# Sparse attention of eight head pairs: the same instructions of three engines in another order

## The reference, cut to what matters

```python
sc = jnp.einsum('bqghd,bngd->bghqn', qg, k_cmp) * scale              # 31 compressed keys
p_cmp = softmax(where(valid_c, sc, NEG)) * any(valid_c)
o_cmp = jnp.einsum('bghqn,bngd->bqghd', p_cmp, v_cmp)
...
p_sel = softmax(where(valid_s, ss, NEG)); o_sel = p_sel @ v_sel      # causal, keys k_slc
p_w = softmax(where(valid_w, sw, NEG));   o_win = p_w @ v_win        # causal, keys k_win
...
out = jnp.einsum('bsch,bschd->bshd', gates, o).reshape(b, s, NSA_HEADS * DH)
return out @ w_o
```

## Time and profile before

| | |
|---|---|
| three runs | 2616.98, 2619.18, 2621.26 us |
| median | 2619.18 us |
| span of the profiled execution | 2617.9 us (its time is recorded as this span alone) |
| busy in the span | PE 2422.9 (93%), DVE 1367.0 (52%), ACT 988.3 (38%), POOL 1048.6 (40%) |
| the stage, from the first scores to the first product of the output projection | 853.53 to 1036.08 us, 182.6 us |

### The profile page before, as it was taken

One profiled execution on the slowest core, in us unless ns is written; L12 is line 12 of the kernel. 1 busy time (PEld: TensorE's weight loads), 2 busy tenths in 40 slices (PEclk: granted clock), 3 DMA queues, 4 the chain that ended last, 5 costly groups with the idle time before them and its releaser, 6 DMA issues.

```text
span 2617.9 us, 37191 instructions
## 1 busy us (share of the span) xinstructions
PE 2422.9 (93%) x13933; PEld 1920.0 (73%) x13933; DVE 1367.0 (52%) x2006; ACT 988.3 (38%) x1828; POOL 1048.6 (40%) x977
## 2 busy tenths in 40 slices
PE   6999899999999898999999799989999899899995
PEld 5777688888576555788888688869978797555553
DVE  3334254335364775344434656661167642588885
ACT  3344322222211665322223333341145401268784
POOL 7554444444006004544443645435741276401111
PEclk8999999999999999999999899999999899899998
DMA  4111233323233000333331211112210122399996
GB/s 132 57 49 57 84 100 95 98 89 104 65 102 92 1 1 9 104 98 96 96 97 41 77 41 44 47 49 73 81 33 27 31 89 76 130 308 362 366 369 234
DMA packets 267869, 268.51 MB, mean 103 GB/s; under 512 B 13339, under 2 KB 198518, under 8 KB 267750
## 3 DMA queue, kind: packets, MB, share of 16 engines
q1 hardware_dynamic: 262998, 253.91, 30.2%
q0 software_dynamic: 4752, 12.98, 1.9%
HBM read 256.10 MB, written 10.75 MB: 102 GB/s over the span
## 4 chain that ended last, share of the span: by engine, by line
PE 76%; DVE 9%; ACT 6%; DMA 5%; issue 3%; POOL 1%; SPq 0%; DVEq 0%; POOLq 0%; ACTq 0%
PE psum L2745 16%; PE psum L2749 16%; PE psum L2748 16%; DMA ex_tile<-in_w_down 4%; PE psum L1504 3%; PE psum L2388 2%; PE psum L844 2%; PE psum L2454 2%; PE psum L846 2%; PE psum L845 2%; PE psum L2260 1%; PE psum L2397 1%; ACT probs_a L1344 1%; ACT probs_b L1344 1%; PE psum L2265 1%
## 5 line engine op out<-in xcount | busy, mean ns | idle before, releaser
L2745 PE MATMUL psum<-x_hi,w_hi 128*128 128x264 f32 (+1 forms) x1536 | 525.5, 342 | 28.9 <-DVE x_lo L765 18.8
L2748 PE MATMUL psum<-x_lo,w_hi 128*128 128x264 f32 (+1 forms) x1536 | 515.7, 336 | 0.0
L2820 POOL TENSOR_TENSOR w_lo<-ring_tile,w_hi 128x1024 fp32r<-128x1024 f32 x128 | 307.8, 2406 | 381.1 <-ACT w_hi L2803 379.0
L803 POOL TENSOR_TENSOR w_hi<-ring_tile,one 128x256 fp32r<-128x256 f32 (+1 forms) x284 | 233.3, 848 | 484.9 <-PE psum L2749 450.3
L2745 PEld LDWEIGHTS psum<-x_hi,w_hi 128*128 128x128 f32 x1536 | 292.5, 190 | 65.9 <-issue 31.3
L2749 PE MATMUL psum<-x_hi,ring_tile_lo 128*128 128x264 f32 (+1 forms) x1088 | 340.2, 313 | 0.0
L2748 PEld LDWEIGHTS psum<-x_lo,w_hi 128*128 128x128 f32 x1536 | 292.9, 191 | 29.2 <-issue 1.2
L807 POOL TENSOR_TENSOR ring_tile_lo<-ring_tile,w_hi 128x256 fp32r<-128x256 f32 (+1 forms) x284 | 296.8, 1072 | 8.2
L3051 DVE TENSOR_TENSOR h<-psum,h 128x512 f32<-128x512 f32 x80 | 55.0, 692 | 337.3 <-PE psum L2749 270.1
L2803 ACT ACTIVATE w_hi<-ring_tile 128x1024 fp32r<-128x1024 f32 x128 | 135.0, 1057 | 251.6 <-PE psum L2749 240.9
L2749 PEld LDWEIGHTS psum<-x_hi,ring_tile_lo 128*128 128x128 f32 x1088 | 206.9, 190 | 11.8
(11 more groups left out here) (428 smaller groups left out, 5243.5 us busy)
## 6 DMA issues: line engine op xcount, KB each, us to landing
ring_tile<-in_mlp_w SPq DMA_DIRECT2D x128, 512.0 KB, 3.9
ex_tile<-in_w_gate SPq DMA_DIRECT2D x64, 512.0 KB, 12.6
ex_tile<-in_w_up SPq DMA_DIRECT2D x64, 512.0 KB, 12.2
ex_tile<-in_w_down SPq DMA_DIRECT2D x64, 512.0 KB, 12.0
ring_tile<-in_w_in SPq DMA_DIRECT2D x52, 512.0 KB, 3.8
ring_tile<-in_sb_w_qkv SPq DMA_DIRECT2D x24, 512.0 KB, 3.8
ring_tile<-in_nsa_w_kv SPq DMA_DIRECT2D x12, 512.0 KB, 3.6
ring_tile<-in_sb_w_o SPq DMA_DIRECT2D x8, 512.0 KB, 3.6
```

What stands on the lines that cost most here:

```text
L803: last = pool.tensor_tensor(hi[:, cols], raw[:, cols], one[:, :].broadcast_to([P, D // len(parts)]), ALU.mult)
L2745: upper = pe.matmul(dst, a_hi, b_hi, start=first, stop=False)
L2748: pe.matmul(dst, a_hi, b_lo, start=False, stop=False)
L2820: pool.tensor_tensor(lo, raw, hi.bitcast(F32), ALU.subtract).then_inc(split_w, 1)
```

## The change

No instruction is added or removed. The order of the stage changes in all three queues:

- PE: a unit starts with first scores sooner (ahead of F0 in a selection unit, behind F0 in a window unit), and the second scores stand ahead of F2 in a selection unit and ahead of F3 in a window unit. The next pair's compressed scores move from the window unit to the selection unit, between C1 and the second weighing. `cmp_weigh` moves from the end of the selection unit to the window unit, behind F4.
- ACT: the second take of the compressed branch moves behind the next unit's first exponentials, and `cmp_exps` behind the second ones.
- DVE: both maxima of the next unit stand ahead of the normalisation of this one, with `factor` made before them (a function of its own, `nsa_factor`). `cmp_normalise` comes after `nsa_out` and `factor` in a window unit, and `cmp_softmax` first in a selection unit.
- The slots' numbers follow (`fill_slot`, `cmp_slot`, `slot_taken`): compressed scores are now slot 13u-5 and no longer 13u-3.

```diff
--- before.py
+++ after.py
@@ -1189,10 +1189,10 @@
             return PER_PAIR * u + (len(FILLS) - 1, len(FILLS) + 1)[hh]
 
         def fill_slot(f):
-            return f + 1 + min((f + 3) // PER_PAIR, NSA_PAIRS - 1)
+            return f + 1 + min((f + 5) // PER_PAIR, NSA_PAIRS - 1)
 
         def cmp_slot(u):
-            return SLOTS_PER_PAIR * u - 3 if u else 0
+            return SLOTS_PER_PAIR * u - 5 if u else 0
 
         def slot_bank(s):
             return bank[5 + s % 2]
@@ -1202,11 +1202,11 @@
             was = s - 2
             if was < 0:
                 return
-            u = (was + 3) // SLOTS_PER_PAIR
+            u = (was + 5) // SLOTS_PER_PAIR
             if was == 0 or (was == cmp_slot(u) and u < NSA_PAIRS):
                 pe.wait_ge(cmp_blk, cmp_no(u if was else 0))
             else:
-                pe.wait_ge(ns_t, was - min((was + 2) // SLOTS_PER_PAIR, NSA_PAIRS - 1))
+                pe.wait_ge(ns_t, was - min((was + 4) // SLOTS_PER_PAIR, NSA_PAIRS - 1))
 
         def score_bank(hh, i):
             return (bank[4][:, 256 * hh:256 * hh + 256], bank[hh][:, :])[i // 2] if i % 2 else (
@@ -1307,33 +1307,39 @@
             nsa_scores(pe, 1, 1)
             for d in range(UNITS):
                 u, slc, more = d // 2, d % 2 == 0, d + 2 < UNITS
-                nsa_fill(pe, d, 0)
-                nsa_fill(pe, d, 1)
-                if more:
-                    nsa_scores(pe, d + 2, 0)
-                if not slc and more:
-                    cmp_scores(pe, u + 1)
-                nsa_fill(pe, d, 2)
                 if slc:
+                    if more:
+                        nsa_scores(pe, d + 2, 0)
+                    nsa_fill(pe, d, 0)
+                    nsa_fill(pe, d, 1)
+                    if more:
+                        nsa_scores(pe, d + 2, 1)
+                    nsa_fill(pe, d, 2)
                     nsa_fill(pe, d, 3)
-                if more:
-                    nsa_scores(pe, d + 2, 1)
-                if slc:
                     cmp_fill(pe, u, 0)
+                    nsa_fill(pe, d, 4)
                 else:
+                    nsa_fill(pe, d, 0)
+                    if more:
+                        nsa_scores(pe, d + 2, 0)
+                    nsa_fill(pe, d, 1)
+                    nsa_fill(pe, d, 2)
+                    if more:
+                        nsa_scores(pe, d + 2, 1)
                     nsa_fill(pe, d, 3)
-                nsa_fill(pe, d, 4)
+                    nsa_fill(pe, d, 4)
+                    cmp_weigh(pe, u)
                 pe.wait_ge(ns_t, fill_at(d, 3) + 1)
                 if slc and u:
                     pe.wait_ge(ns_oe, u)
                 nsa_weigh(pe, d, (0, 2))
                 if slc:
                     cmp_fill(pe, u, 1)
+                    if more:
+                        cmp_scores(pe, u + 1)
                 pe.wait_ge(ns_t, fill_at(d, 4) + 1)
                 last = nsa_weigh(pe, d, (1, 3))
-                if slc:
-                    cmp_weigh(pe, u)
-                else:
+                if not slc:
                     last.then_inc(ns_o, 1)
 
         def nsa_exps(act, d, k):
@@ -1372,17 +1378,17 @@
                 u, slc, more = d // 2, d % 2 == 0, d + 1 < UNITS
                 if more:
                     nsa_exps(act, d + 1, 0)
+                if not slc:
+                    cmp_take(act, u, 1)
+                if more:
+                    nsa_exps(act, d + 1, 1)
                 if slc:
                     cmp_exps(act, u)
-                if more:
-                    nsa_exps(act, d + 1, 1)
                 for k in range(4):
                     nsa_take(act, d, k)
                 if slc:
                     cmp_take(act, u, 0)
                 nsa_take(act, d, 4)
-                if slc:
-                    cmp_take(act, u, 1)
 
         def nsa_maxima(dve, d, k):
             dve.wait_ge(ns_s, score_no(d, k))
@@ -1414,12 +1420,14 @@
             step(dve, dve.tensor_tensor(cmp_s[:, :, :], cmp_s[:, :, :], cmp_any[:, :].unsqueeze(1).broadcast_to([P, 2, QT]), ALU.mult))
             dve.tensor_tensor(flat, flat, sums.unsqueeze(2).broadcast_to([P, 2 * QT, N_CMP]), ALU.mult).then_inc(cmp_hh, 1)
 
+        def nsa_factor(dve, d):
+            dve.wait_ge(ns_p, piece_no(d, 1))
+            fac = factor[:, d % 2, :, :]
+            step(dve, dve.reciprocal(fac, rsum[:, d % 2, :, :]))
+            step(dve, dve.tensor_tensor(fac, fac, gate_of(d // 2, 1 + d % 2), ALU.mult))
+
         def nsa_normalise(dve, d):
             b = d % 2
-            dve.wait_ge(ns_p, piece_no(d, 1))
-            fac = factor[:, b, :, :]
-            step(dve, dve.reciprocal(fac, rsum[:, b, :, :]))
-            step(dve, dve.tensor_tensor(fac, fac, gate_of(d // 2, 1 + d % 2), ALU.mult))
             for hh in range(2):
                 for i in reversed(range(QT)):
                     rows = probs[b][hh][:, PROB_AT[i]:PROB_AT[i] + P * (i + 1)]
@@ -1437,17 +1445,17 @@
                 nsa_maxima(dve, 0, k)
             for d in range(UNITS):
                 u, slc, more = d // 2, d % 2 == 0, d + 1 < UNITS
+                if slc:
+                    cmp_softmax(dve, u)
+                elif u:
+                    nsa_out(dve, u - 1)
+                nsa_factor(dve, d)
                 if not slc:
                     cmp_normalise(dve, u)
-                    if u:
-                        nsa_out(dve, u - 1)
                 if more:
-                    nsa_maxima(dve, d + 1, 0)
-                if slc:
-                    cmp_softmax(dve, u)
+                    for k in range(2):
+                        nsa_maxima(dve, d + 1, k)
                 nsa_normalise(dve, d)
-                if more:
-                    nsa_maxima(dve, d + 1, 1)
             nsa_out(dve, NSA_PAIRS - 1)
 
 
```

## The result

The changed kernel takes 2597.06 us (median of four, 2593.92 to 2607.24), before 2620.22 (2616.98 to 2622.94, the three of before and one beside them): ratio 0.9916, 95% interval 0.9902 to 0.9929. That is 23 us less, where 13.7 were forecast; the time lies under the range of 2601.5 to 2613. Two executions of all that follow, 2811 us (kernel before) and 3385 us (PE's and ACT's order), ran at a granted clock of 0.82 and 0.67 and are left out of every comparison.

A forecast was written before the change was run, and what follows sets the result against it. PE was taken to bound the kernel (76% of the chain), idling 2.12 us a pair, mostly for ACT. Six pairs by 1.93 (11.6), start 2.4 and end -0.3 made 13.7 us, so 2605.5 us; range 2601.5 to 2613.

The forecast's parts named there:

- I take the difference off the median: Whole kernel: the stage's summed gain of 13.7 us is subtracted from the median time, giving 2605.5 us.
- The steady part: Six pairs of units in the changed stage: 1.93 us gained a pair, 11.6 us in all.
- the ladder: One pair's new order, summed from PE's start-to-start lengths and queue positions: 19.30 us, taken as 19.2.
- The stall of 0.08 before F4: Selection unit: F4 on PE waits 0.08 us for T3 on ACT to free its slot.
- The start: First units of the stage: 2.4 us gained if the clock stays up, 0.7 if it falls.
- The end: Last pair, beside POOL: 2.3 us longer from the last second scores, net 0.3 us lost.
- best bound: Stage without stall or overcount: 2.4 us by 6, start 2.4, end 1 better; some 18 us, 2601.
- The last sentence of the prediction: Signs of error: window F2 waits over 0.5 us, F0 waits for DVE, or stage shrinks 14 us without the time.
- shorter waits don't cost clock: PE's clock: it was 1.00 through waits of 1 us, so the start's shorter waits keep it up.
- hold F2: Rival, window unit: exponentials 1 us late on ACT delay F2; gain 7.7 us, 2611.5; chance 0.20.
- the second maxima in front of the normalisation: Slower rival, F0 of each unit: uncovered maxima delay PE, 11 us lost in six pairs, 2630; chance 0.10.
- the rule on the port pair: Last pair: DVE and POOL share an exclusive port lock, so each of eight scalings waits out one POOL instruction.

The follow-up runs named there:

- only_PD: PE's and DVE's new orders with ACT's order as before, against the kernel before: 20.20 us a pair, ratio 0.9982.
- 6 products: The changed kernel plus 6 unused PE products (1.4 us of work, no delay) behind the last weighing: median 2606.69 us.
- 31 products, POOL late: The changed kernel with POOL's first four weight splits waiting for the last normalisation, plus 31 unused PE products behind the last weighing: 2605.48 us.
- 11 products: The changed kernel plus 11 unused PE products (1.0 us of delay) behind the last weighing: 2609.81 us.
- 16 products: The changed kernel plus 16 unused PE products (2.1 us of delay) behind the last weighing: 2599.03 us.

## Why the prediction was right or wrong

The time is outside the range because the sum stopped at the end of the changed stage. The step that failed is "I take the difference off the median": it puts what the stages behind win or lose at nothing. They took 10 to 11 us less (1547.1 and 1547.8 for 1558.0 and 1557.9 in the two traces of each kernel). That the stage's own gain came out near the forecast is in part luck, as its errors cancel. Within the stage its terms came out so:

- *The steady part*, 1.93 us a pair: measured 2.25, 13.5 us for 11.6. The mechanism was right: one stall left, before C0 for T2, 0.25 us for the forecast 0.31, and F2 of the window unit follows without a wait. The size was off in the first scores, 1.17 in the ladder and 1.02 in the trace, twice in a pair, since they were read from a row whose end is modelled; and in the first weighing with C1, 2.00 in the ladder and 1.90 in the trace (947.38 to 949.28). The stall of 0.08 before F4 is too short to be listed, but C0 with F4 takes 1.07 us (946.31 to 947.38), where it took 0.96.
- *The start*, 2.4 us: measured 1.3 (24.39 us from the first scores to F0 of unit 1, for 25.73). The waits are 1.15 and 0.83, forecast 1.4 and 0.8, but the clock fell all the same (0.74 from 864.0 to 870.5). The forecast was for a clock that stays up; the 1.3 lie between its 2.4 and the 0.7 given for the case that it falls (rows below the list).
- *The end*, -0.3: measured -2.1 (32.13 for 30.05). The wait for C0 was 3.23 for 3.3, and a head beside POOL 2.8 to 3.1. The half clock was priced at 1.7 us lost; from C0 to F0 of the last unit it took 6.75 us (1006.19 to 1012.94) for 3.97 at full speed, so 2.8 lost. Of the other 0.7 us, 0.4 had come up by C0, which starts 12.7 us behind the last second scores and not 12.3.
- *Together* 12.8 for 13.7: the steady part gave 1.9 us more than forecast, the start and the end 1.1 and 1.8 less, so the errors cancel.
- *The range* had as its best bound the stage alone, 18 us; it left no room for what the stages behind may win. The last sentence of the prediction names the opposite case alone, a stage that shrinks while the time doesn't.

The waits of PE at the start of the changed stage, and the window behind them:

```profile
859.96 0.45 PE L1226 MATMUL psum<-k_hi,qr_hi 64*128 64x256 f32 x2 [1.71 <-ACT probs_b L1350]
...
863.15 0.50 PE L1226 MATMUL psum<-k_hi,qr_hi 64*128 64x512 f32 x2 [1.15 <-ACT probs_b L1350]
...
865.16 1.82 PE L1281 MATMUL psum<-ident,probs_a 128*128 128x128 f32 x8 [0.83 <-DVE probs_a L1434]
```

```profile
864.00:870.50 6.50, 5.67 (x44) 4.73 (x42) 5.86 (x18) 3.70 (x13) 0.00 (x0) 0.74 0.00 0
```

So "shorter waits don't cost clock", in the prediction's paragraph on the clock, is wrong: it fell behind waits of 1.71, 1.15 and 0.83 us, while it stayed at 1.00 through the single waits of the earlier trace rows. Nor are single waits safe: with PE's order alone it stayed up in some pairs and fell in others, with one wait of 1.7 us in each.

The rivals: ACT doesn't hold F2 (no such wait), and the second maxima in front of the normalisation cost nothing with the three orders together. The place where ACT could hold F2 was rightly picked: in `only_PD` the take of C1 in front of the exponentials holds PE there for 1.2 us a pair.

By the rule on the port pair (the Trainium skill, SBUF — State Buffer, "SBUF: two separate sides") a scaling waits out a POOL instruction; the trace agrees, 3.05 us beside POOL and 1.26 without it for the same four instructions. That is 0.45 us more for each, where one of POOL's beside it takes 0.58 to 0.75. Not all of DVE's instructions are longer there: the three maxima take 1.89 us with and without POOL and a reciprocal 0.2, but the product of `factor` with the gates takes 0.53 for 0.17. A lock of the port isn't shown by itself, only that taking POOL away gives the time back.

**What stays open.** Shown is that the lengths behind the stage go with the time that PE spends at half clock, and that kernels which differ by 1 to 2 us of work ahead differ in it, with the same work behind. Not shown is what in the start's place decides: counted from the span's start, starts at 1021.8 and 1023.7 us (6 products) gave the short lengths and one at 1022.7 (31 products, POOL late) the long ones, and executions of one kernel fall on both sides. Why the changed kernel falls on the good side in seven of eight, and the kernel before on the long side in all but one of its 102, was not settled. So of the 23 us some 13 are the change's own, and 10 are had by this build as it stands.

## What to carry to other kernels

Reorder all queues together: here PE's order alone moved the wait to DVE, with DVE's it went to ACT, and the sum of the single gains is less than half of the joint one. A ladder from start-to-start rows gave the last of these waits, 1.2 us, before it was seen. Before a gain is put down to an edit, compare the stages that it doesn't touch; where they differ with the same instructions and another granted clock, add different amounts of useless work, of a microsecond or so, and see if the gain stays in all of them: here 11 products lost it in six executions of six, and 16 kept it in four of seven.

## What the hardware showed that was not expected

Stages with the same instructions took 251.9, 255.7 or 257.0 us (grouped heads), 435.4 to 441.9 (differential heads) and 77.4 to 80.5 us (output and norm), each with its own granted clock. The clock came back after 3.4 us in one kernel and after 13.7 us in the other, behind the same products and waits. Seven microseconds less in one stage (162.6 for 169.8) made the program no faster, and 1.8 us more made it 13.6 us slower (2609.81 for 2596.18, 11 products), while 1.9 us more made it 2.9 us slower (2599.03, 16 products). An interval from many runs of a kernel doesn't cover this, since it comes out otherwise for the same work after a shift. A difference of 13 us, 0.5% of this kernel, can't be given to an edit by the whole time alone.
